# Norm stages shared over three more hands, and two stages of products in the seven-product form

## The reference

```python
def rmsnorm(x, g):
    x32 = x.astype(jnp.float32)
    y = x32 * lax.rsqrt(jnp.mean(x32 * x32, axis=-1, keepdims=True) + EPS)
    return (y * g.astype(jnp.float32)).astype(x.dtype)

def modulate(x, g, shift, scale):
    return rmsnorm(x, g) * (1 + scale) + shift

def conv_ffn(h, w_up, conv_w, conv_b, w_down):
    u = dwconv_centred(h @ w_up, conv_w, conv_b)     # depthwise, 3 taps along the tokens
    a, b = u[..., :D_FF], u[..., D_FF:]              # D_FF = 2816
    return (jax.nn.silu(a) * b) @ w_down
```

## Time and profile before

| | us |
|---|---|
| median of three runs (5511.56 to 5519.2) | 5513.02 |
| profiled execution, its own time | 5505.79 |
| its span, first to last instruction | 5503.8 |
| TensorE busy | 4832.0 (88%) |
| VectorE busy | 2418.1 (44%) |
| ScalarE busy | 1202.7 (22%) |
| GpSimd busy | 762.6 (14%) |
| mean granted TensorE clock | 0.935 |

### The profile page before, as it was taken

How to read it: one execution, slowest core, us unless ns; L and a number is a source line. 1 busy time by engine, 2 the same in 40 slices (tenths; PEclk the granted TensorE clock), 3 DMA queues, 4 the chain that set the end, 5 groups by cost and what they waited for, 6 DMA issues and landing times.

```text
span 5503.8 us, 69798 instructions
## 1 busy us (share of the span) xinstructions
PE 4832.0 (88%) x28286; PEld 2839.3 (52%) x28286; DVE 2418.1 (44%) x4071; ACT 1202.7 (22%) x2143; POOL 762.6 (14%) x942
## 2 busy tenths in 40 slices
PE   6977887889999999999879943899888999999998
PEld 3555734554454434455445522789744444455446
DVE  2446843441243212377566578355633444332114
ACT  2112412330011001111010154222212344301120
POOL 0003400000000000011000047656100000000000
PEclk9988998889999999999989965899999999999999
DMA  3312141012112120244112255444211000022122
GB/s 143 100 60 92 39 164 46 33 39 92 61 69 77 70 83 31 98 152 163 69 36 95 89 179 208 109 105 112 81 44 47 26 35 35 16 92 77 61 73 77
DMA packets 152344, 451.07 MB, mean 82 GB/s; under 512 B 73184, under 2 KB 73440, under 8 KB 130784
## 3 DMA queue, kind: packets, MB, share of 16 engines
q1 hardware_dynamic: 129184, 354.39, 18.8%
q0 software_dynamic: 22848, 92.29, 4.8%
HBM read 377.42 MB, written 69.21 MB: 81 GB/s over the span
## 4 chain that ended last, share of the span: by engine, by line
PE 62%; issue 11%; DVE 7%; POOLq 7%; PEld 6%; DMA 2%; ACT 2%; DVEq 2%; POOL 1%; PEldq 0%; SPq 0%; ACTq 0%
PE psum L386 51%; PEld psum L386 5%; POOLq L2576 3%; POOLq L2574 2%; PE psum L2138 2%; PE psum L2137 2%; PE psum L648 1%; PE psum L2108 1%; DVE sbuf L1091 1%; PE psum L1274 1%; DVE sbuf L663 1%; DVE sbuf L1388 1%; PE psum L1242 1%; PEld psum L1849 1%; PE psum L1029 1%
## 5 line engine op out<-in xcount | busy, mean ns | idle before, releaser
L386 PE MATMUL psum<-sbuf 128*128 128x512 f32 (+4 forms) x9632 | 3390.7, 512 | 200.2 <-DVE sbuf L1578 51.1
L386 PEld LDWEIGHTS psum<-sbuf 128*128 128x128 f32 (+1 forms) x9632 | 1793.4, 192 | 1754.2 <-issue 1479.0
L3176 PE MATMUL psum<-sbuf 64*64 64x64 f32 (+1 forms) x10752 | 426.0, 237 | 29.7 <-SPq L3085 17.6
L3176 PEld LDWEIGHTS psum<-sbuf 64*64 64x64 f32 x10752 | 411.1, 138 | 46.9 <-SPq L3085 19.3
L598 DVE CUSTOM_DVE_ANT_0 sbuf<-sbuf 128x1024 f32<-128x1024 f32 x160 | 212.8, 1330 | 34.5 <-DMA sbuf<-w_side 18.2
L2771 PE MATMUL psum<-sbuf 64*128 64x512 f32 (+2 forms) x192 | 85.8, 707 | 143.1 <-ACT sbuf L2845 65.6
L1590 DVE SCALAR_TENSOR_TENSOR sbuf<-psum,sbuf 128x256 f32<-128x256 f32 (+2 forms) x288 | 125.7, 479 | 192.4 <-PE psum L386 187.7
L3301 ACT ACTIVATE sbuf<-psum 128x256 f32<-128x256 f32 (+3 forms) x384 | 128.6, 368 | 362.2 <-PE psum L3176 301.7
L679 DVE TENSOR_SCALAR sbuf<-sbuf 128x512 f32<-128x512 f32 (+1 forms) x68 | 36.2, 533 | 355.0 <-ACT sbuf L1649 200.7
L631 ACT ACTIVATE sbuf<-sbuf 128x512 f32<-128x512 f32 (+1 forms) x114 | 53.0, 551 | 616.7 <-DVEq L3475 599.5
L588 POOL DMA_DIRECT2D sbuf<-w_side x128 | 68.4, 535 | 860.4 <-DVE sbuf L598 859.7
(11 more groups left out here) (287 smaller groups left out, 4905.9 us busy)
## 6 DMA issues: line engine op xcount, KB each, us to landing
sbuf<-w_side POOLq DMA_DIRECT2D x128, 512.0 KB, 3.8
sbuf<-w_sgu_uz SPq DMA_DIRECT2D x32, 1088.0 KB, 5.4
sbuf<-terms SPq DMA_DIRECT2D x115, 256.0 KB, 2.7
sbuf<-w_up SPq DMA_DIRECT2D x22, 1024.0 KB, 4.8
sbuf<-w_merge SPq DMA_DIRECT2D x8, 2560.0 KB, 9.2
sbuf<-w_mla_head SPq DMA_DIRECT2D x16, 1152.0 KB, 5.1
sbuf<-w_sgu_v SPq DMA_DIRECT2D x8, 2048.0 KB, 7.8
sbuf<-w_sgu_out SPq DMA_DIRECT2D x8, 2048.0 KB, 7.9
```

The costliest lines, as they stand in the source:

```text
L386: last = nc.tensor.matmul(out, w, x, start=(n == 0), stop=(n == len(pairs) - 1))
L3176: last = t.matmul(out[hs], lhs[hs], rhs[hs], start=start, stop=stop)
```

## The change

`Norm`: the even tiles are squared by ScalarE, the odd ones by VectorE. All reciprocals are taken before any scaling. VectorE scales only the first job's tiles; of the other jobs GpSimd multiplies each tile by the reciprocal, and ScalarE applies factor and shift in one activation. In `Residual` and `StrassenResidual` ScalarE, idle there, does one Sqrt on a spare word at the start. `FfnUp` is rewritten in the seven-product form: one stage tile is a tile of each half, with 28 products of 256 columns; ScalarE copies products 2 and 5 into the padded rows, VectorE adds the other five there, convolves a tile after its product 7, and gates it one tile later. `SguMixSeven` does the same for layer 3, with the mixing products after product 4; GELU and SiLU now read SBUF. In the diff `a(...)`, `b(...)`, `quarter(...)`, `a_sum` and `b_sum` are those of `StrassenResidual` for these operands; the head of `SguMixSeven` and the parts that are the same as in `FfnUp` are left out.

```diff
@@ -627,30 +629,52 @@
     def scalar(self, act):
         a = self.nc.scalar
         for job, n, squares, rms, inv, factor, k, t in self.places():
-            for i in range(k):
+            for i in range(0, k, 2):
                 a.activation(squares[:, i], job["x"][:, i], ACT.Square).then_inc(self.squared, 1)
         for job, n, squares, rms, inv, factor, k, t in self.places():
             act.wait_ge(self.summed, n + 1)
             a.activation(rms, self.chip.bank(n, t), ACT.Sqrt, scale=1.0 / (k * P), bias=EPS).then_inc(self.rooted, 1)
         done = 0
         for job, n, squares, rms, inv, factor, k, t in self.places():
-            if job.get("shift") is not None:
+            shift = job.get("shift")
+            if n == 0 and shift is not None:
                 for i in range(k):
-                    act.wait_ge(self.scaled, done + i + 1)
-                    a.activation(job["out"][:, i], job["out"][:, i], ACT.Identity, bias=job["shift"][:, i:i + 1])
-            done += k
+                    act.wait_ge(self.scaled, i + 1)
+                    a.activation(job["out"][:, i], job["out"][:, i], ACT.Identity, bias=shift[:, i:i + 1])
+            if n > 0:
+                act.wait_ge(self.inverted, n + 1)
+                for i in range(k):
+                    act.wait_ge(self.scaled_too, done + i + 1)
+                    if shift is not None:
+                        a.activation(job["out"][:, i], job["out"][:, i], ACT.Identity, bias=shift[:, i:i + 1], scale=factor[:, i:i + 1])
+                    else:
+                        a.activation(job["out"][:, i], job["out"][:, i], ACT.Copy, scale=factor[:, i:i + 1])
+                done += k
 
     def tensor(self, pe):
         done = 0
         for job, n, squares, rms, inv, factor, k, t in self.places():
             for i in range(k):
-                pe.wait_ge(self.squared, done + i + 1)
+                if i % 2 == 0:
+                    pe.wait_ge(self.squared, done + i // 2 + 1)
+                else:
+                    pe.wait_ge(self.squared_too, done + i // 2 + 1)
                 last = self.nc.tensor.matmul(self.chip.bank(n, t), self.chip.const("ones"), squares[:, i], start=(i == 0), stop=(i == k - 1))
             last.then_inc(self.summed, 1)
-            done += k
+            done += k // 2
+
+    def gpsimd(self, pool):
+        for job, n, squares, rms, inv, factor, k, t in self.places():
+            if n > 0:
+                pool.wait_ge(self.inverted, n + 1)
+                for i in range(k):
+                    self.nc.gpsimd.tensor_tensor(job["out"][:, i], job["x"][:, i], inv, ALU.mult).then_inc(self.scaled_too, 1)
 
     def vector(self, dve):
         v = self.nc.vector
+        for job, n, squares, rms, inv, factor, k, t in self.places():
+            for i in range(1, k, 2):
+                v.tensor_tensor(squares[:, i], job["x"][:, i], job["x"][:, i], ALU.mult).then_inc(self.squared_too, 1)
         for job, n, squares, rms, inv, factor, k, t in self.places():
             if job.get("scale") is None:
                 v.tensor_copy(factor, job["gain"])
...
+        dve.drain()
         for job, n, squares, rms, inv, factor, k, t in self.places():
             dve.wait_ge(self.rooted, n + 1)
-            v.reciprocal(inv, rms)
-            dve.drain()
-            for i in range(k):
-                v.scalar_tensor_tensor(job["out"][:, i], job["x"][:, i], factor[:, i:i + 1], inv, ALU.mult, ALU.mult).then_inc(self.scaled, 1)
+            v.reciprocal(inv, rms).then_inc(self.inverted, 1)
+        dve.drain()
+        job, n, squares, rms, inv, factor, k, t = next(self.places())
+        for i in range(k):
+            v.scalar_tensor_tensor(job["out"][:, i], job["x"][:, i], factor[:, i:i + 1], inv, ALU.mult, ALU.mult).then_inc(self.scaled, 1)
...
+    def scalar(self, act):
+
+        spare = self.chip.view(A_SMALL + 508, 1)
+        self.nc.scalar.activation(spare, self.chip.const("ones")[:, 0:1], ACT.Sqrt)
...
-        for i in range(0, KF // 2):
-            for u in range(2):
-                self.w.landed(pe, i, u)
-                pe.wait_ge(self.copied, 2 * i + u + 1)
-                w = self.w.view(u, 2, KD, P)
-                for n in range(2):
-                    last = products(self.nc, self.chip.bank(2 * u + n), [(w[:, n, k], self.h[:, k]) for k in range(KD)])
-                last.then_inc(self.w.used(u), 1)
+        S = StrassenResidual
+        for j in range(KF):
+            self.w.landed(pe, j // 2, j % 2)
+            for i, n in enumerate(self.PRODUCTS):
+                if n in S.A_SUMS:
+                    pe.wait_ge(self.a_ready, 5 * j + S.A_ORDER.index(n) + 1)
+                    w = self.a_sums[n]
+                else:
+                    w = self.a(j, *S.A_PLAIN[n])
+                if n in S.B_PLAIN:
+                    x = self.b(*S.B_PLAIN[n])
+                else:
+                    x = self.b_sums[n]
+                    if j == 0:
+                        pe.wait_ge(self.b_ready, S.B_ORDER.index(n) + 1)
+                if j > 0:
+                    if n in (2, 5):
+                        pe.wait_ge(self.first, 2 * (j - 1) + (2, 5).index(n) + 1)
+                    else:
+                        pe.wait_ge(self.added, 5 * (j - 1) + i - 1)
+                products(self.nc, self.chip.bank(i, self.WIDTH), [(w[:, k], x[:, k]) for k in range(self.HALF)]
+                         ).then_inc(self.products_done, 1)
+            pe.drain().then_inc(self.w.used(j % 2), 1)
...
+        def silu(j):
+            act.wait_ge(self.convolved, j + 1)
+            a.activation(self.acc[j % 2][0], self.acc[j % 2][0], ACT.Silu, bias=self.chip.vec("ffn_b", j, 1)
+                         ).then_inc(self.activated, 1)
...
+            if j >= 2:
+                act.wait_ge(self.convolved, j - 1)
+            for i, n in enumerate((2, 5)):
+                act.wait_ge(self.products_done, 7 * j + i + 1)
+                for half, part, sign in S.RESULTS[n]:
+                    last = a.activation(self.quarter(j, half, part), self.chip.bank(i, self.WIDTH), ACT.Copy, scale=float(sign))
+                last.then_inc(self.first, 1)
+            if j >= 1:
+                silu(j - 1)
+        silu(KF - 1)
...
+        def convolve(j):
+            for n in range(2):
+                last = conv3(self.nc, dve, self.acc[j % 2][n], self.raw[j % 2][n],
+                             [self.chip.vec("ffn_w", 2 * KF * k + KF * n + j, 1) for k in range(3)], TL)
+            last.then_inc(self.convolved, 1)
+
+        def gate(j):
+            dve.wait_ge(self.activated, j + 1)
+            v.scalar_tensor_tensor(self.g[:, j], self.acc[j % 2][1], self.chip.vec("ffn_b", j + KF, 1), self.acc[j % 2][0],
+                                   ALU.add, ALU.mult).then_inc(self.gated, 1)
+
+        for n in (2, 5):
+            a_sum(0, n)
+        for n in S.B_ORDER:
+            b_sum(n)
+            if n in S.A_SUMS:
+                a_sum(0, n)
         for u in range(2):
             for n in range(2):
-                v.memset(self.raw[u][n], 0.0)
+                last = v.memset(self.raw[u][n], 0.0)
         dve.drain().then_inc(self.padded, 1)
-        for i in range(0, KF // 2):
-            for u in range(2):
-                j = 2 * i + u
-                dve.wait_ge(self.copied, j + 3)
-                dve.wait_ge(self.gated, j + 1)
-                for n in range(2):
-                    last = conv3(self.nc, dve, self.acc[u][n], self.raw[u][n],
-                                 [self.chip.vec_at("ffn_w", 2 * KF * k + KF * n + j) for k in range(3)], TL)
-                last.then_inc(self.convolved, 1)
-            for u in range(2):
-                j = 2 * i + u
-                dve.wait_ge(self.activated, j + 1)
-                dve.wait_ge(self.convolved, j + 3)
-                v.scalar_tensor_tensor(one(self.g, j), self.acc[u][1], self.chip.vec_at("ffn_b", j + KF), self.acc[u][0],
-                                       ALU.add, ALU.mult).then_inc(self.gated, 1)
+        for j in range(KF):
+            for i, n in enumerate(self.PRODUCTS):
+                dve.drain()
+                if n == 2:
+                    dve.wait_ge(self.products_done, 7 * j + 1)
+                elif n == 5:
+                    dve.wait_ge(self.first, 2 * j + 2)
+                else:
+                    dve.wait_ge(self.products_done, 7 * j + i + 1)
+                    for half, part, sign in S.RESULTS[n]:
+                        quarter = self.quarter(j, half, part)
+                        last = v.tensor_tensor(quarter, quarter, self.chip.bank(i, self.WIDTH), ALU.add)
+                    last.then_inc(self.added, 1)
+                if j + 1 < KF and n in S.A_SUMS:
+                    a_sum(j + 1, n)
+                if n == 3 and j >= 1:
+                    gate(j - 1)
+            dve.drain()
+            convolve(j)
+        dve.drain()
+        gate(KF - 1)
...
+class SguMixSeven(Stage):
...
```

(79 more changed lines are left out.)

137 lines of the change are left out of this document (124 added, 13 removed).

## The result

The changed kernel takes 5476.87 us in the median of five runs (5462.09 to 5484.97), the kernel before 5511.56 (five runs, 5492.53 to 5519.2); the ratio is 0.994, with a 95% interval of 0.9913 to 0.9966. That is 34.7 us less, where 30.7 were forecast. The profiled execution of the changed kernel has a span of 5460.1 us, its own time is 5462.09.

A forecast was written before the change was run, and what follows sets the result against it. TensorE, busy 88% of the span, was taken to bound the product stages. FFN -25.0, layer 3 mix -23.7, norms with context +18.4 and rank norm -0.4 gave -30.7 us, from 5513.0 to 5482.3; range 5463 to 5495.

The forecast's parts named there:

- FFN tile: FFN stage: a tile goes from 13.76 to 12.62 us, bound by TensorE; the stage changes by -25.0 us.
- VectorE's sum: FFN stage: VectorE's work per tile is 11.9 to 12.5 us, just under TensorE's 12.62.
- Mix stage: Layer 3 mix stage: a tile goes from 15.15 to 13.59 us; the stage changes by -23.7 us.
- Squares: Norm stages: halving ScalarE's squares gives 0, as TensorE's sums bound; layer 1's root table load gives -0.4 us.
- Scaling: Norms with a context (input, layers 0, 1, 2): GpSimd and VectorE collide, +4.7 us per norm.
- Rank norm: Norm of three jobs without shift: from 14.9 to 14.5 us, -0.4.
- (B): Rival: GpSimd and VectorE don't hinder each other in the norms; some 5465 us, chance 0.12.
- (C): Rival: norms cost more, pairs of 1.5 us and a colder TensorE afterwards; 5490 to 5496 us, chance 0.11.
- (D): Rival: VectorE becomes the bound of the FFN stage; 5490 to 5500 us, chance 0.08.
- (E): Rival: the FFN convolution doesn't hide, tile 16.8 us; 5574 us in all, chance 0.04.
- (F): Rival: seven products don't shorten the tiles, only the norms are felt; 5531 us, chance 0.02.

The follow-up runs named there:

- ffn_two_more: Changed kernel with two extra VectorE products of 128x512 ahead of each FFN tile's convolution; 5505.13 us, ratio 0.9988 to the kernel before.
- seven_only: Changed kernel with the norm stages of before, keeping both seven-product stages and the early Sqrt; 5464.44 us, ratio 0.9911 to the kernel before.
- gpsimd_later: Changed kernel, but GpSimd starts the other jobs' tiles only after VectorE has scaled the first job's; single time 5458.14 us.
- inv_in_psum: Changed kernel, but the first job's reciprocal goes to a PSUM bank, where VectorE's scaling reads it; 5464.59 us, ratio 0.9916 to the kernel before.
- ctx_on_vector: inv_in_psum with the context's factor and shift as one VectorE operation per tile instead of ScalarE activations; 5449.48 us, ratio 0.989 to the kernel before.

## Why the prediction was right

- **FFN tile.** 12.62 forecast from the `w_out1` tile, 12.62 measured. The form had to be the same, not the stage. The slow first tile was over-counted: I left its 2.9 us as they were, and it took 14.25 against 12.36, 1.9 more. That is most of the 1.4 by which the stage came out shorter. The rest: TensorE starts 0.96 behind the norm where it started 0.31 behind it, 0.65 more and not 0.9; the tail is 6.64 and was reckoned as 6.7.
- **VectorE's sum.** 11.9 to 12.5 forecast, 12.0 measured through `ffn_two_more`. The wait for product 7 was to be some tenths and is 0.28 in the tile shown. Of the waits with 5 to 9 us of slack, the one that gives way first is that for the weight sum of the next tile's first product and not `added`: the lag of 0.94 a tile (13.56 less 12.62) reached it after five tiles, 4.7 us.
- **Mix stage.** 13.59 forecast, 13.52 measured: the mixing products take 0.89 between products 3 and 4 (5148.32 to 5149.21) for 0.97. The tail grew by 0.5, as reckoned. The start grew by 2.4 where I had 0.8: in the eight profiles with this stage the first product's weights land 6.0 to 8.4 us behind ScalarE's table load, in the kernel after 7.5. The first tile gave 1.2 back, 1.8 us slower than the others where it had been 2.9 slower.
- **Squares.** 0 forecast, 0 shown in the norm of layer 2, where it was tested. The table load in layer 1 was worth 0.15 at the root, not 0.4: 8.02 us from the first square before, 7.87 after, and 7.87 too in `seven_only`, which has all squares on ScalarE and the early Sqrt.
- **Scaling.** +4.7 per norm forecast, +4.6 from the root on measured in each of the four. The mechanism was right; that the number is so close is luck, since two errors cancel. Eight pairs take 9.2 us and not 9.8. Single instructions were sized well, GpSimd's 0.73 (`gpsimd_later`) for 0.74 and VectorE's 0.75; it is the overlap that was too small, 0.34 a pair (0.73 + 0.75 - 1.13) and not 0.26. Part of that was in the row already: 1.81 + 0.96 - 2.48 is 0.29 and not twice 0.13. On the other side, ScalarE's context block takes 4.02 where I carried over 3.30 from an activation without a scale operand.
- **Rank norm.** -0.4 forecast, -0.9 measured. From the first reciprocal on it takes 13.9 us, where I had 14.5.
- **Rivals.** (B), no collision, is out by the 9.19 of the scalings; `inv_in_psum` shows that it needs another operand. (C), dearer norms and a colder TensorE behind them, did not occur: a pair takes 1.13 and not 1.5, and the 96 records behind the norm of layer 2 take 43.85 us, where they took 44.51. (D), VectorE as the bound of the FFN stage, and (E), a convolution that does not hide, did not occur either; `ffn_two_more` puts the decision point for (D) at 0.6 us of added VectorE work per tile and shows that (E)'s full serial price is not what happens even beyond it. (F), no shorter tiles, is out by the tile of 12.62. A slip without effect: the chances of (E) and (F) add up to 0.06, not 0.05.

## What to carry to other kernels

Work that is handed to an idle engine is worth nothing where another engine ends the phase (the squares), and less than nothing where it needs what the busy engine needs (the context tiles). Look for a place in the trace where the two already overlap, read what the pair costs, and put that into the sum. Where GpSimd must run beside VectorE, try one VectorE input in PSUM: for the two operations tested here it took the collision away. Before work of a stage is moved from TensorE to VectorE, add up VectorE's work for a tile against TensorE's tile, and lay out by hand which wait has how much slack. The sum says whether TensorE will be held up, and the slack says from which tile on.

## What the runs showed of the hardware

- In a row of eight, a ScalarE activation of 256 columns takes 0.41 us with a bias column alone (3.30 for eight) and 0.50 with a scale column too (4.02 for eight). I had not expected the operand to cost 0.09.
- The GpSimd product of two tiles of 256 float32 columns takes 0.73 us alone, and eight in a row 5.52 (`gpsimd_later`); beside VectorE with an input from PSUM eight take 5.57 (`inv_in_psum`).
- VectorE's scaling with one input from PSUM takes 0.67 us a tile beside GpSimd (5.36 for eight), the same as with two SBUF inputs and GpSimd idle (5.39).
- Executions of one kernel differ by up to 30 us (`ctx_on_vector`, 5437.04 to 5466.62), and the stretch from layer 1's norm to layer 2's, with nothing edited but that one Sqrt, by 17 between profiles. With such a spread a change of 10 us is seen in the stage, not in the total.
